# A decoder block on one core: 22 weight remainders made by ScalarE's negative and an accumulating transfer

## What is computed

```python
def peer(xn, w_query, sub_keys, expert_u, expert_v):          # 512 tokens, width 1024
    q = (xf @ w_query).reshape(t, 8, 2, 128)                  # 8 heads, two half queries
    scores = jnp.einsum('thpk,hpnk->thpn', q, sub_keys)       # 128 keys for each half
    v1, i1 = lax.top_k(scores[:, :, 0], 16)
    v2, i2 = lax.top_k(scores[:, :, 1], 16)
    cand = (v1[..., :, None] + v2[..., None, :]).reshape(t, 8, 256)
    best, pos = lax.top_k(cand, 16)
    experts = (e1 * 128 + e2)                                 # of 16384 experts, 128 for each token
    gates = softmax(best)
    a = gelu(xn . expert_u[experts]) * gates
    return sum over the experts of a * expert_v[experts]

def reference(x, ...):
    xn = rmsnorm(h, norm_mix_g); h = h + hybrid_mixer(xn, ...)   # short convolution, pooling, gates
    xn = rmsnorm(h, norm_ffn_g); h = h + peer(xn, ...)
    return rmsnorm(h, norm_final_g)
```

## Time and profile before

| | |
|---|---|
| median of 3 runs | 1697.04 us (1696.98 to 1697.32) |
| the profiled execution | 1697.09 us, its span 1695.3 us |
| granted TensorE clock, mean | 0.996 |
| busy: PE, DVE, ACT, POOL | 1679.1, 1299.1, 673.6, 289.9 us |
| DMA, mean over the span | 245 GB/s |

### The profile page before, as it was taken

How to read it: one execution, slowest core, us unless ns; L and a number is a source line. 1 busy time by engine, 2 the same in 40 slices (tenths; PEclk the granted TensorE clock), 3 DMA queues, 4 the chain that set the end, 5 groups by cost and what they waited for, 6 DMA issues and landing times.

```text
span 1695.3 us, 27470 instructions
## 1 busy us (share of the span) xinstructions
PE 1679.1 (99%) x9711; PEld 1575.4 (93%) x9711; DVE 1299.1 (77%) x2303; ACT 673.6 (40%) x882; POOL 289.9 (17%) x267
## 2 busy tenths in 40 slices
PE   9999999999999999999999999999999999999997
PEld 7888888888889999999999999999999999999997
DVE  6855533335559999999999997777788888888885
ACT  5322433334334333344665656333333333333332
POOL 0000000000000100022222222432133333333330
PEclk9999999999999999999999999999999999999998
DMA  4322322222323665578988998988899999999981
GB/s 174 122 91 98 124 89 97 99 90 97 112 75 108 237 222 199 207 264 303 343 325 320 325 327 323 395 339 303 316 335 395 358 374 377 363 381 359 363 313 60
DMA packets 122021, 415.38 MB, mean 245 GB/s; under 512 B 13680, under 2 KB 16752, under 8 KB 120304
## 3 DMA queue, kind: packets, MB, share of 16 engines
q1 hardware_dynamic: 75168, 232.59, 38.3%
q0 software_dynamic: 36864, 134.23, 22.0%
q10 hardware_dynamic: 9936, 47.98, 7.1%
HBM read 366.25 MB, written 48.50 MB: 245 GB/s over the span
## 4 chain that ended last, share of the span: by engine, by line
PE 86%; DVE 10%; issue 3%; DMA 0%; ACT 0%; DVEq 0%; SPq 0%; ACTq 0%
PE bank L783 16%; PE bank L785 16%; PE bank L784 16%; PE bank L942 11%; PE bank L943 11%; PE bank L941 11%; PE bank L925 4%; DVE w_lo L985 1%; DVE less L1253 1%; DVE top_i L1260 1%; DVE rows L1350 1%; DVE top_i L1252 1%; DVE top_v L1257 1%; DVE top_v L1249 1%; DVE found L1316 1%
## 5 line engine op out<-in xcount | busy, mean ns | idle before, releaser
L985 DVE TENSOR_TENSOR w_lo<-w_raw,w_hi 128x1024 fp32r<-128x1024 f32 x347 | 424.0, 1222 | 214.4 <-ACT w_hi L510 203.4
L510 ACT ACTIVATE w_hi<-w_raw 128x1024 fp32r<-128x1024 f32 x347 | 366.2, 1056 | 465.3 <-PE bank L943 325.3
L783 PE MATMUL bank<-xn_hi,w_hi 128*128 128x384 f32 (+1 forms) x1472 | 522.7, 355 | 3.2 <-DVE w_lo L985 3.2
L785 PE MATMUL bank<-xn_hi,w_lo 128*128 128x384 f32 (+1 forms) x1472 | 517.5, 352 | 0.0
L784 PE MATMUL bank<-xn_lo,w_hi 128*128 128x384 f32 (+1 forms) x1472 | 516.9, 351 | 0.0
L941 PE MATMUL bank<-a_hi,w_hi 128*128 128x384 f32 x1024 | 348.5, 340 | 0.0
L942 PE MATMUL bank<-a_lo,w_hi 128*128 128x384 f32 x1024 | 347.9, 340 | 0.0
L943 PE MATMUL bank<-a_hi,w_lo 128*128 128x384 f32 x1024 | 347.8, 340 | 0.0
L472 POOL DMA_INDIRECT rows<-u_rows,expert x128 | 146.4, 1143 | 1050.9 <-DVE expert L1376 550.3
L783 PEld LDWEIGHTS bank<-xn_hi,w_hi 128*128 128x128 f32 x1472 | 276.4, 188 | 21.7 <-issue 4.6
L784 PEld LDWEIGHTS bank<-xn_lo,w_hi 128*128 128x128 f32 x1472 | 276.6, 188 | 17.7 <-issue 0.2
(11 more groups left out here) (190 smaller groups left out, 1388.4 us busy)
## 6 DMA issues: line engine op xcount, KB each, us to landing
w_raw<-u SPq DMA_DIRECT2D x128, 512.0 KB
w_raw<-v SPq DMA_DIRECT2D x128, 512.0 KB
g_dram<-g_sb ACTq DMA_DIRECT2D x12, 2048.0 KB
g_in<-g_dram SPq DMA_DIRECT2D x84, 256.0 KB
act_dram<-act_out ACTq DMA_DIRECT2D x54, 384.0 KB, 4.3
act_in<-act_dram SPq DMA_DIRECT2D x54, 384.0 KB
w_raw<-gate SPq DMA_DIRECT2D x32, 512.0 KB
w_raw<-w_in SPq DMA_DIRECT2D x31, 512.0 KB
```

The lines of the kernel that those rows point to most:

```text
L510: act.activation(w_hi[:, slot, :], w_raw[:, slot, :], ACT.Copy).then_inc(hi_done, 1)
L783: pe.matmul(out, hi, x_hi, start=k == 0, stop=False)
L785: last = pe.matmul(out, lo, x_hi, start=False, stop=k == NB - 1)
L985: dve.tensor_tensor(w_lo[:, slot, :], w_raw[:, slot, :], w_hi[:, slot, :].bitcast(F32), ALU.subtract).then_inc(lo_done, 1)
```

## The change

For the tiles of `u` in steps 2 to 12 (`SUMMED_FROM` to `SUMMED_TO` - 1) with slot 1 or 3, 22 in all (`N_SUMMED`), DVE makes no `w_lo`. ScalarE writes the negative of the rounded weight into `w_lo`, right after `w_hi`, and GpSimd then issues a transfer that adds the tile's float32 weights from DRAM to it (`accum_op=ALU.add`), so that `w_lo` is again `w_raw - w_hi`. PE waits for that transfer (`lo_summed`, one counter for each of the two slots). The subtractions are fewer by 22, so every later wait on `lo_done` is for a number lower by `N_SUMMED`. SP loads slots 1 and 3 again after the negative (`minus_hi`).

In GpSimd's order the first four gathers stand first; then for each group of four tiles the two sums, followed by as many gathers as the step has dots. The dots of retrieval are 3 in even steps and now 2 in odd steps from 3 on: 25 instead of 15. `ROWS_V` goes from 110 to 120, 8 dots are left for the multiplication with `v`, and the `v` rows begin at tile 12. PE's loop over the steps becomes two steps written out, a loop over steps 2 to 12, and step 13 written out.

```diff
-DOTS_TOPK = 3
+DOTS_TOPK = (2, 3)
...
+SUMMED_FROM, SUMMED_TO = 2, TOPK_STEPS + 1
+N_SUMMED = 2 * (SUMMED_TO - SUMMED_FROM)
+def by_dma(group, b):
+    return isinstance(group, int) and SUMMED_FROM <= group < SUMMED_TO and b % 2 == 1
+def lo_target(group, b, region):
+    if region == 0:
+        return SLOTS * group + (AT_U + b + 1)
+    if region == 1:
+        return 2 * group + (AT_U + 2 * SUMMED_FROM + b // 2 + 1)
+    return SLOTS * group + (AT_U + b + 1 - N_SUMMED)
...
+            def load_u(group, region):
+                for b in range(SLOTS):
+                    if region == 1 and b % 2 == 1:
+                        sp.wait_ge(minus_hi, 2 * group + (b // 2 - 2 * SUMMED_FROM - 1))
+                    else:
+                        sp.wait_ge(lo_done, lo_target(group - 1, b, region))
+                    load_slot(u_d, SLOTS * group + b, b)
...
-            for r in range(PAIRS):
+            def gather_u(r):
                 if r >= ROW_SLOTS:
                     pool.wait_ge(rows_used, r - ROW_SLOTS + 1)
                 pool.sem_inc(wait_carried, 1)
                 gather(u_rows, r, r % ROW_SLOTS)
+            def sum_lo(group, b):
+                pool.wait_ge(minus_hi, 2 * (group - SUMMED_FROM) + b // 2 + 1)
+                pool.dma_start(w_lo[:, b, :], u_d[SLOTS * group + b], accum_op=ALU.add).then_inc(lo_summed[b // 2], 16)
+            started = ROW_SLOTS
+            for r in range(ROW_SLOTS):
+                gather_u(r)
+            for group in range(SUMMED_FROM, SUMMED_TO):
+                for b in (1, 3):
+                    sum_lo(group, b)
+                count = DOTS_TOPK[group % 2] if group - 1 >= 2 else 0
+                for r in range(started, started + count):
+                    gather_u(r)
+                started += count
...
                 split_weight(SLOTS * step + (AT_U + SLOTS + b), b, step + (AT_U // SLOTS + 2))
+                if summed and b % 2 == 1:
+                    act.activation(w_lo[:, b, :], w_raw[:, b, :], ACT.Copy, scale=-1.0).then_inc(minus_hi, 1)
...
+            def u_tile(step, b, parts=None, region=2):
+                lo = (lo_done, lo_target(step, b, region))
+                if region == 1 and b % 2 == 1:
+                    lo = (lo_summed[b // 2], 16 * step + 16 * (1 - SUMMED_FROM))
...
-                split_weight(SLOTS * step + (AT_U + SLOTS + b), b)
+                if not by_dma(step + 1, b):
+                    split_weight(SLOTS * step + (AT_U + SLOTS + b), b)
...
-                    u_dots(rows_done, DOTS_TOPK)
-                    rows_done += DOTS_TOPK
...
+                if n >= 2:
+                    count = DOTS_TOPK[(n + 1) % 2]
+                    u_dots(rows_done, count)
+                    rows_done += count
...
-            first_row = SLOTS + dots_left + 2
+            first_row = SLOTS * ((SLOTS + dots_left - 1) // SLOTS + 1)
```

More of the change, by code:

```diff
@@ L101 @@
 DOTS_PLAIN = (2, 2, 1, 2)
-ROWS_V = (DOTS_TOPK * (TOPK_STEPS // 2 - 1) + sum(DOTS_BEFORE) + ROUNDS * sum(DOTS_ROUND)
+ROWS_V = (sum(DOTS_TOPK) * (TOPK_STEPS // 2 - 1) + sum(DOTS_BEFORE) + ROUNDS * sum(DOTS_ROUND)
           + (U_STEPS - 1 - PLAIN_AT) * sum(DOTS_PLAIN))
@@ L322, in build @@
         lo_done = sem("lo_done")
+        minus_hi = sem("minus_hi")
+        lo_summed = [sem(f"lo_summed{k}") for k in range(SLOTS // 2)]
         job_done = sem("job_done")
@@ L381, in load_raw, with load_slot @@
             def load_raw(source, k, n, slot):
-                if not isinstance(n, int) or n >= SLOTS:
+                if isinstance(n, int) and n < SLOTS:
+                    pass
+                elif isinstance(n, int) and n - SLOTS >= AT_U + SLOTS * SUMMED_TO:
+                    sp.wait_ge(lo_done, n - SLOTS + 1 - N_SUMMED)
+                else:
                     sp.wait_ge(lo_done, n - SLOTS + 1)
+                load_slot(source, k, slot)
+            def load_slot(source, k, slot):
                 sp.dma_start(w_raw[:, slot, :], source[ds(k), :, :].rearrange("o p d -> (o p) d")
                              ).then_inc(raw_loaded[slot], 16)
+            def load_u(group, region):
+                for b in range(SLOTS):
+                    if region == 1 and b % 2 == 1:
+                        sp.wait_ge(minus_hi, 2 * group + (b // 2 - 2 * SUMMED_FROM - 1))
+                    else:
+                        sp.wait_ge(lo_done, lo_target(group - 1, b, region))
+                    load_slot(u_d, SLOTS * group + b, b)
             def load_all(source, first, count, start=0):
@@ L416, in load_g @@
                     at += end - begin
-            load_all(u_d, AT_U, KEYS - N_PIECES)
+            for group in range(SUMMED_FROM + 1):
+                load_u(group, 0)
+            with sp.Fori(SUMMED_FROM + 1, SUMMED_TO + 1) as group:
+                load_u(group, 1)
+            with sp.Fori(SUMMED_TO + 1, (KEYS - N_PIECES) // SLOTS) as group:
+                load_u(group, 2)
             for k in range(2):
@@ L483, in _ @@
                 gather(u_rows, r, r % ROW_SLOTS)
+            def sum_lo(group, b):
[11 more added lines that the diff above has]
+                started += count
+            for r in range(started, PAIRS):
+                gather_u(r)
             for r in range(PAIRS):
@@ L651, in _, with gelu_tile @@
                 act.activation(x_tok[:, k * T:(k + 1) * T], bank[4 + k][:], ACT.Copy).then_inc(x_tok_ready, 1)
-            def gelu_tile(step, b):
+            def gelu_tile(step, b, summed=False):
                 act.wait_ge(job_done, SLOTS * step + (AT_U + b + 1))
@@ L697, in _ @@
                 gelu_tile(0, b)
-            with act.Fori(1, TOPK_STEPS) as step:
+            with act.Fori(SUMMED_FROM - 1, SUMMED_TO - 1) as step:
                 for b in range(SLOTS):
-                    gelu_tile(step, b)
+                    gelu_tile(step, b, summed=True)
             for b in range(SLOTS // 2):
@@ L742, in v_group @@
                     split_a(SLOTS * g + b, b)
-            gelu_dots_at = (SLOTS + PAIRS - ROWS_V) // SLOTS
+            gelu_dots_at = (SLOTS + PAIRS - ROWS_V - 1) // SLOTS
             for g in range(1, gelu_dots_at + 1):
@@ L766, in tile_product @@
             def tile_product(n, b, uses, act_hi, act_lo, parts=None, base=0, tokens=slice(0, T), used=None,
-                             halves=False):
+                             halves=False, lo=None):
                 if halves:
                     pe.wait_ge(half_lo, 1)
+                elif lo is not None:
+                    pe.wait_ge(*lo)
                 else:
@@ L890, in _ @@
             score(last_group, SLOTS - 1)
[L892 to L897, removed]
+            def u_tile(step, b, parts=None, region=2):
+                lo = (lo_done, lo_target(step, b, region))
+                if region == 1 and b % 2 == 1:
+                    lo = (lo_summed[b // 2], 16 * step + 16 * (1 - SUMMED_FROM))
+                tile_product(SLOTS * step + (AT_U + b), b, step + (USES_U + 1), xn_hi, xn_lo, parts, NB, tokens=DENSE,
+                             lo=lo)
+            for step in range(SUMMED_FROM):
+                for b in range(SLOTS):
+                    u_tile(step, b, xn_l if step == 0 and b == 0 else None, region=0)
+            with pe.Fori(SUMMED_FROM, SUMMED_TO) as step:
+                for b in range(SLOTS):
+                    u_tile(step, b, region=1)
+            for step in range(SUMMED_TO, ONEHOT_AT - 1):
                 for b in range(SLOTS):
@@ L934, in v_ready @@
             def v_ready(g, b):
-                pe.wait_ge(lo_done, SLOTS * g + (AT_V + b + 1))
+                pe.wait_ge(lo_done, SLOTS * g + (AT_V + b + 1 - N_SUMMED))
                 pe.wait_ge(al_ready, SLOTS * g + (b + 1))
```

## The result

The changed kernel takes **1705.63 us** (median of 5, 1704.58 to 1707.78) against 1696.99 (1696.93 to 1697.32): 1.005 times, 95% interval 1.0039 to 1.0062. It is 0.5% slower. It lies in the range that I gave, but not where I put it: 8.6 us above the 1697.0, and on the slower side, which had 0.35.

A forecast was written before the change was run, and what follows sets the result against it. PE was taken as the bound, busy 99%, with only small holes to win. From the profiled 1697.09 us, -4.2 for DVE's holes and +4.0 for the first sum's wait gave 1696.9, said as 1697.0; range 1692.8 to 1712.

The forecast's parts named there:

- DVE's four holes: Four step turns in retrieval where PE waits for DVE's `w_lo`; all were to go, -4.2 us.
- the ten dots beside v: Ten dots leave the multiplication with v, where PE waits for nothing: 0.
- the price of a dot: DVE's cost of each dot added in retrieval: 1.14 us, 11.4 us for ten.
- the first wait: PE's wait at step 2, slot 1, for the first sum, queued behind four gathers: +4.0 us, once.
- SP's loads [...]: 0: Loads of slots 1 and 3, waiting for the negative, hide behind the 12 us until ScalarE wants them: 0.
- 0.22 MB/us: Rate of GpSimd's software queue beside the loads, used to price a sum's 0.52 MB as a copy: 2.4 us.
- At double price: 5.6: Upper bound in us for PE's wait for the first sum, against 3.2 as a copy.
- Rival D: The clock falls in the one wait for the first sum: 1696 to 1701, say 1698.5; chance 0.10.
- this leaves about 1 us: Room left for steady-state sums behind two or three gathers, at a double price.
- B: Rival: additions fill the DMA engines in retrieval; 1702 near the threshold, up to 1729; chance 0.22.
- inside 8.3: A steady-state sum lands in 3.9 us as a copy, 6.3 at twice the data cost, within the 8.3 us left.
- B's threshold of 2.1 copies: Cost of one sum at which a retrieval step's bytes stop fitting the DMA engines: 2.1 copies.

The follow-up runs named there:

- e9_one_slot_spread: Changed kernel with only slot 1 summed (11 sums), no dots more, first sum ahead of gathers, two of each three gathers behind the next sum: 1693.09 us.
- e1_first_sums: Changed kernel with the first sum issued ahead of the first gathers, two gathers between it and the sum of slot 3: 1698.34 us.
- e3_dots_only: Kernel before the change with the ten more dots in retrieval and no sums by transfer: 1709.94 us.
- e10_late_load: Changed kernel with SP's load of slot 1 waiting for DVE's split of slot 2, not for ScalarE's negative: 1704.41 us.
- e2_copy: Changed kernel with the addition left out, so GpSimd's 22 transfers copy the weight into `w_lo`: 1702.35 us.
- e5_spread: Changed kernel with the first sum ahead of the gathers and one or two of each step's gathers behind the next slot-1 sum: 1694.12 us.
- e8_first_no_dots: Changed kernel with the first sum ahead of the gathers and without the ten more dots in retrieval: 1696.49 us.
- e7_warm: Changed kernel with 24 products of ones on PE ahead of step 2, slot 1, the first awaited tile: 1706.48 us.

## Why the prediction was wrong

*Right:* DVE's four holes go, -4.2 (with the waits for sums gone too, `e9_one_slot_spread` is 4.20 us shorter). ScalarE's negatives, GpSimd's issue (0.91 us each), the ten dots beside v and DVE's wait for their GELU cost nothing. The place of the main wait and its cause, four gathers ahead in one queue, were right: with the sum ahead of them the wait is gone (`e1_first_sums`). So was the price of a dot (`e3_dots_only`).

*Wrong in size: the first wait, 4.0 taken, bounds 1.5 to 5.6, measured 8.1.* Three parts failed. First, "SP's loads [...]: 0": the load that comes 3 us early falls among the gathers, and held back to 563.25 it makes the wait 2.1 us shorter (`e10_late_load`). Second, the rate: I gave the sum the 0.22 MB/us that gathers had from 560 to 563. But it shares the engines with the loads of the next tiles, and with the sum of slot 3 behind it. The software queue of the changed kernel from 566, 570 and 574 us on, one us each:

```profile
q0 software_dynamic: 50, 0.17, 64.4%
...
q0 software_dynamic: 38, 0.13, 63.8%
...
q0 software_dynamic: 21, 0.05, 27.0%
```

At 0.13 MB/us 0.52 MB take 4 us. Third, the kind: an addition is 1.7 copies of engine time, which in this place is 1.4 us (7.95 against 6.58 in `e2_copy`). The upper bound, "At double price: 5.6", doubled a copy priced too low; that it was no bound is shown by the copy itself, which waits 6.6.

*Wrong by leaving it out of the sum: the clock.* Rival D had 0.10 and 1.4 us. It fell in every kernel that kept the long wait, and here it cost 2.5. By the tail of the earlier trace rows it fell within four us after the dense work; a forecast of 4.0 us of waiting should have carried it. The Trainium skill's rule that I had cited, throttled by default and released by activity ("TensorE: Matmul & The Clock Gate", Part 1), is in agreement with the 0.50 from 568 to 578 us.

*Wrong: "this leaves about 1 us".* The five later sums behind three gathers were late by 0.3 to 1.7 us, 3.9 in all. I had them as the near end of B (1702) and gave nothing in the sum. The step that failed is "inside 8.3": the landing is 8.3 us in the median and 13.4 at most, not 3.9 to 6.3. B's threshold of 2.1 copies is not tested. At 1.7 its sum of bytes fills (3.96 + 1.7 x 1.05) / 6.14 of the 0.97, which is 0.91; the three queues above add up to 0.99. The engines are full before the bytes say so, and single sums are late while PE loses little in all (`e5_spread`).

So 4.1 for the first wait, 2.5 for the clock and 3.9 for the later sums were missing, 10.5 in all in the profiled execution (the medians differ by less, 8.6), against a gain of 4.2 that could never carry them.

## What to carry to other kernels

Before a producer is moved to a queue, look at what lies in that queue when its first transfer is issued, and price the transfer by a landing under the same load, never by its bytes. Weigh the size of the prize: where a bound engine has 4 us of holes, take just enough work off the other engine (11 of 22 subtractions did it) and put what is awaited ahead of what is not. An idle stretch of PE of a few us can cost more than itself, since the clock comes back late: 8.1 us of waiting cost 2.5 more here.

## What was not expected of the hardware

- An accumulating transfer of 512 KB from DRAM into SBUF costs the 16 engines about 2.6 us against 1.5 for the copy (`e2_copy`), and lands in 8.3 against 6.7 us in the median beside loads and gathers. GpSimd needs 0.85 to 1.01 us to issue it.
- A wait of 2.3 us was once followed by a fall of the granted clock to 0.50 (`e8_first_no_dots`), and after 2.0 us of idle it fell when dense matmuls had already begun again (`e7_warm`). In `e3_dots_only` waits of 2.00 and 1.80 us were followed by a fall too, and one of 2.12 us was not; nor was one of 2.00 us at 710 us in `e7_warm`. The length of a wait alone does not tell. Waits of 1.0 to 1.4 us brought no fall in the kernel before and the changed one.
- A share of 1.01 of the DMA engines did not stall PE where the order was right (`e5_spread`).
